# Scores of two query tiles in one group, and one PSUM bank each for the transposed probabilities and the value products

## The chip, the cores and the metric

The kernel runs on one core of a Trainium2 chip. A core has five engines that work from queues of their own: PE (TensorE: matrix products and transposes), DVE (VectorE), ACT (ScalarE), POOL (GpSimd) and SP (which issues DMAs). Each executes its instructions in order and waits on semaphores that the others raise. PE writes into PSUM, eight banks of 128 partitions by 512 float32 values; ACT and DVE read it. The metric is the device time of one execution in microseconds.

## The reference

One decoder layer on a sequence of 512 tokens and 1,024 channels. Of it the change touches the attention alone:

```python
ilog = einsum('bqhd,bsd->bqhs', qib, ki)                # indexer: which 128 keys a query keeps
_, sel = lax.top_k(iscore, topk)
s = einsum('bqhd,bqkhd->bhqk', qb, kg) * scale          # 8 heads of 64
s = s - slopes[None, :, None, None] * dist[:, None]     # ALiBi
p = jax.nn.softmax(s, axis=-1)
return einsum('bhqk,bqkhd->bqhd', p, vg)
```

Before it stand the modulated norm and the input projections, after it the gates, the output projection and a gated MLP.

## The kernel before

All large products are done in float32 parts: a weight is split by ACT into a high part (L805) and by POOL into a low part (L721), and a product is two high products and one low product for each block of 128 rows.

**The attention loop.** The 512 queries are four tiles of 128 (i = 0 to 3). Tile i sees (i + 1) x 128 keys. The heads are taken in four pairs. A step is one head and one tile; there are 32. The loop `for t in range(SLOTS)` stands in the programs of PE, ACT and DVE, and one turn of it is called a slot here. `ORDER` puts the steps of a pair as tile 0, 0, 1, 1, 3, 3, 2, 2, the two heads in turn. What one step needs is spread over slots:

- PE, slot t: at the first slot of a pair the scores of tiles 0 and 1 of both heads (twelve products), at its fifth those of tile 3 (six), at its seventh those of tile 2 (six). `scored_with` says which, and PE waits for `logit_ok` of step t-1 before them. A score product contracts over 64 rows, so the two heads of a pair take one half of the array each. Both heads' scores go to `SC`, banks 3 and 4.
- DVE, slot t: adds the scores to the linear term (L1419), which leaves the row's maximum; then the bias of the exponential (L1423); then, for step t-1, the division by the sum (L1430).
- ACT, slot t: the linear term of step t+1 (L979), the exponential of step t (L1010, which waits for the bias and, since `prob` has three places, for the transposes of step t-3), and the copy of the transposed probabilities of step t-3 from PSUM to `pT` (L1018).
- PE, slot t: transposes the probabilities of step t-3 (L1857), i + 1 of 128 x 128, into `PT[(t - 3) % 2]`, banks 5 and 6 in turn. It waits for the copy of step t-5, the last reader of that bank.
- PE, slot t, last: a filler, which is a part of a projection that has nothing to do with the step. Even slots do the high products and odd slots the low ones: 16 and 8 products of 512 columns for the fillers `gp` and `ga`, 8 and 4 for `pb`. Their banks are 0 and 1. The order is gp in slots 0 to 3, pb 4 to 7, gp 8 to 11, pb 12 to 15, gp 16 to 19, pb 20 to 27, ga from 28.
- ACT, at the end of every even slot: after the filler's last product, the high split of the weight three fillers ahead (L805) and, for gp and ga, a tanh (L926, L993).
- PE, slots 11, 19, 27 and 35: `head_products`, the value products of a pair, into `HEADS`, which is bank 7 (OB) for pairs 0 and 2 and bank 2 for pairs 1 and 3. They are read in the slot after by ACT (L1000) and DVE (L1278).

```python
HEADS = (OB, banks[2])
return {0: (0, 1), 4: (3,), 6: (2,)}.get(r, ())   # scored_with, r = t % 8
pe.wait_ge(pt_ok, t - 4)                          # before the transposes of slot t
```

Bank 2 belongs to the ring of banks of the projections before the loop (its last user is the first gp product) and after it. Bank 6 is also the last of the four that take the spread norm of the keys before the loop (`k_turn`, `kn_ok`).

Of the kernel before, what the change touches and what calls it, by code (L numbers as in the profile page):

```python
# [8 lines left out]
ACT = mybir.ActivationFunctionType  # L9
AX_X = mybir.AxisListType.X  # L10

P = 128
S, D, FF = 512, 1024, 2816
H, HD = 8, 64
# [4 lines left out]
NT = S // P  # L19
# [74 lines left out]
def scored_with(t):  # L94

    r = t % (2 * NT)
    return {0: (0, 1), 4: (3,), 6: (2,)}.get(r, ())


def scores_by(t):  # L100
# [5 lines left out]
def score_columns(i):  # L106

    return slice(P, 3 * P) if i == 1 else slice(0, (i + 1) * P)
# [163 lines left out]
def build_layer(nc, x, c, w_ada, b_ada, norm1_g, w_in, q_norm_g, k_norm_g, w_attn_br, w_pool_grp, pool_scale,  # L272
                w_pool_br, w_out, norm2_g, w_up, conv_w, conv_b, w_down, out):
    sch = schedule()
    drained_count = []
# [14 lines left out]
    with ExitStack() as ctx:  # L290
# [59 lines left out]
        qT = arena("qT", [P, 2, KA, S], F32R, 0)  # L350
        kT = arena("kT", [P, 2, KA, S], F32R, 16)
        vS = arena("vS", [P, NT, H, HD], F32, 32)
# [25 lines left out]
        logit = arena("logit", [P, 2, S], F32, 93)  # L378
# [27 lines left out]

        banks = [ctx.enter_context(nc.psum_tensor(f"bank{n}", [P, S], F32)) for n in range(8)]
        SC, PT, OB = banks[3:5], banks[5:7], banks[7]
        HEADS = (OB, banks[2])
        SUMS = ((OB, OB), SC)  # L410
        TURN = ((SC[1], PT[0]), (PT[1], OB))

        def gate_banks(n):

            return PT if n else (OB, banks[sch.bank[sch.chunk["wo", 1, 2]]])


        def accumulator(j):
            return {3: macc_rows, 4: macc_gain}.get(j, macc)
# [370 lines left out]
        def _(act):  # L790
# [205 lines left out]
            for t in range(SLOTS):  # L996
                if finished(t) is not None:
                    m = finished(t)
                    act.wait_ge(pv_ok, 2 * (m + 1))
                    me.did(act.activation(qT[:, 0, m, :], HEADS[m % 2][:, :], ACT.Copy), head_hi)  # L1000
                if t < STEPS:
                    if t + 1 < STEPS:
                        alibi_terms(t + 1)
                    h, i = step_of(t)
                    n = (i + 1) * P
                    act.wait_ge(bias_ok, t + 1)
                    if t >= 3:
                        act.wait_ge(prob_t, t - 2)
                    r = i * 2 * H + h
                    me.did(act.activation(prob[:, t % 3, 0:n], logit[:, t % 2, 0:n], ACT.Exp,  # L1010
                                          bias=sbias[:, t:t + 1], scale=stat[:, 2, r:r + 1],
                                          accum_out=ssum[:, t:t + 1]), exp_ok)
                if 3 <= t < STEPS + 3:
                    h, i = step_of(t - 3)
                    act.wait_ge(prob_t, t - 2)
                    if h >= 2:
                        act.wait_ge(pv_ok, 2 * (h // 2))
                    me.did(act.activation(pT[h % 2][:, 0:i + 1, i * P:(i + 1) * P],  # L1018
                                          PT[(t - 3) % 2][:, 0:(i + 1) * P].rearrange("p (j n) -> p j n", n=P),
                                          ACT.Copy), pt_ok)  # L1020
                if t and filler(t - 1)[1] == "low":
                    kind, m = filler(t - 1)[0]
                    if kind == "gp":
                        pool_gate(m)
                    if kind == "ga":
                        gate(m)
                    if kind == "pb":
                        chunk((kind, m))
# [121 lines left out]
        def _(dve):  # L1150
# [126 lines left out]
            def low_of(out_ap, full, hi, signal):  # L1277
                me.did(dve.tensor_tensor(out_ap, full, hi.bitcast(F32), ALU.subtract), signal)  # L1278
# [134 lines left out]
            for t in range(SLOTS):  # L1413
                if t < STEPS:
                    h, i = step_of(t)
                    n = (i + 1) * P
                    dve.wait_ge(linear, t + 1)
                    dve.wait_ge(score, scores_by(t))
                    me.did(dve.tensor_tensor_reduce(logit[:, t % 2, 0:n], logit[:, t % 2, 0:n], SC[t % 2][:, score_columns(i)],  # L1419
                                                    1.0, TAKEN, ALU.add, ALU.max, smax[:, t:t + 1]), logit_ok)  # L1420
                    me.settle()
                    r = i * 2 * H + h
                    me.did(dve.tensor_scalar(sbias[:, t:t + 1], smax[:, t:t + 1], stat[:, 2, r:r + 1], -1.0,  # L1423
                                             ALU.mult, ALU.mult), bias_ok)
                if 1 <= t < STEPS + 1:
                    n = (step_of(t - 1)[1] + 1) * P
                    dve.wait_ge(exp_ok, t)
                    me.did(dve.reciprocal(sinv[:, t - 1:t], ssum[:, t - 1:t]))
                    me.settle()
                    me.did(dve.tensor_scalar(prob[:, (t - 1) % 3, 0:n], prob[:, (t - 1) % 3, 0:n],  # L1430
                                             sinv[:, t - 1:t], None, ALU.mult), prob_ok)
                if finished(t) is not None:
                    m = finished(t)
                    dve.wait_ge(head_hi, m + 1)
                    low_of(qT[:, 1, m, :], HEADS[m % 2][:, :], qT[:, 0, m, :], head_lo)
                if t and filler(t - 1)[1] == "low" and filler(t - 1)[0][0] == "pb":
                    name = filler(t - 1)[0]
                    m = name[1]
                    await_chunk(dve, name)
                    dve.wait_ge(drained["act"], drained_count[sch.chunk["gp", m]][1])  # L1440
                    me.did(dve.scalar_tensor_tensor(out=ypool[:, m, :], in0=ypool[:, m, :], scalar=1.0,
                                                    in1=bank(name)[:, :], op0=ALU.add, op1=ALU.mult),
                           drained["dve"])
# [141 lines left out]
        def _(pe):  # L1585
# [228 lines left out]
            def head_products(m):  # L1814

                pe.wait_ge(pt_ok, 2 * NT * (m + 1))
                if m == 1:
                    who, n = drained_count[max(k for k in range(sch.chunk[FILLERS[0]]) if sch.bank[k] == 2)]
                    pe.wait_ge(drained[who], n)
                if m >= 2:  # L1820
                    pe.wait_ge(head_lo, m - 1)
                for j in range(NT):
                    for e in range(2):
                        mm = pe.matmul(HEADS[m % 2][e * HD:(e + 1) * HD, j * P:], vS[:, j, 2 * m + e, :],  # L1824
                                       pT[e][:, j, j * P:], start=j == 0, stop=j == NT - 1)
                        if j == NT - 1:
                            mm.then_inc(pv_ok, 1)

            for t in range(SLOTS - 1):
                if pair_products(t) is not None:  # L1830
                    head_products(pair_products(t))
                if t < STEPS and scored_with(t):

                    h = step_of(t)[0]
                    if t % (2 * NT) == 0:
                        pe.wait_ge(k_lo, h // 2 + 1)
                    if t == 0:
                        pe.wait_ge(kn_ok, 2)
                    else:
                        pe.wait_ge(logit_ok, t)  # L1840
                    for i in scored_with(t):
                        for a, b in THREE:
                            for e in range(2):
                                r = slice(e * HD, (e + 1) * HD)
                                mm = pe.matmul(SC[e][:, score_columns(i)], qT[r, a, h // 2, i * P:(i + 1) * P],  # L1845
                                               kT[r, b, h // 2, 0:(i + 1) * P], start=(a, b) == (0, 0), stop=a == 1)
                                if a == 1:
                                    mm.then_inc(score, 1)
                if 3 <= t < STEPS + 3:
                    i = step_of(t - 3)[1]  # L1850
                    pe.wait_ge(prob_ok, t - 2)
                    if t < 5:
                        pe.wait_ge(kn_ok, t)
                    else:
                        pe.wait_ge(pt_ok, t - 4)
                    for j in range(i + 1):
                        mm = pe.transpose(PT[(t - 3) % 2][:, j * P:(j + 1) * P],  # L1857
                                          prob[:, (t - 3) % 3, j * P:(j + 1) * P], ident[:, :])
                    mm.then_inc(prob_t, 1)
                if filler(t) and t < STEPS + 3:  # L1860
                    name, part = filler(t)
                    if part == "high":
                        await_bank(pe, name)
                    (high_products if part == "high" else low_products)(
                        sch.unit[name], bank(name), mix if name[0] == "pb" else hT)
# [123 lines left out]
```

## Time and profile before

| | |
|---|---|
| median of 3 runs | 734.26 us (734.16 to 734.49) |
| the profiled execution | 733.26 us |
| its span, first to last instruction | 731.4 us |
| PE busy | 715.4 us (98%) |
| DVE, ACT, POOL busy | 384.6, 307.1, 300.1 us |
| granted TensorE clock, mean | 0.997 of full speed |
| attention loop on PE | about 162.4 to 270.1 us of the span |

Busy PE is time between the start of a product and its modelled end; the gap from the start of one group to the start of the next says what the group really costs. In a timeline the first number is a start in us from the span's beginning, the second how long the group took, and a bracket holds the idle time before it and what ended it.

### The profile page before, as it was taken

The numbers are of one execution on the slowest core, as the hardware profiler recorded it, in microseconds if no ns is written. First come the engines' busy times: TensorE is split into PE (matmuls) and PEld (weight loads), VectorE is DVE, ScalarE is ACT, GpSimd is POOL, SyncE is SP. The second block draws the span as 40 slices with busy tenths as digits, with TensorE's granted clock in tenths as the row PEclk, the third lists the DMA queues.
The fourth block names the chain that finished last, engine by engine and source line by source line (L and its number), as shares of the span: only waits on it lengthen the run. The fifth ranks groups of instructions, "written<-read, shape, count | busy, mean of one in ns | idle before, by whom it ended". The sixth has DMA issues, their size and how long they took to land.

```text
span 731.4 us, 9316 instructions
## 1 busy us (share of the span) xinstructions
PE 715.4 (98%) x3440; PEld 577.6 (79%) x3440; DVE 384.6 (53%) x706; ACT 307.1 (42%) x507; POOL 300.1 (41%) x159
## 2 busy tenths in 40 slices
PE   5899999999999999999999999999999999999997
PEld 4667688877777778887898888887888888888886
DVE  3558899965366616798855445555434432004002
ACT  6325532567577633352636344343334343121120
POOL 1001448826242325473316445444334434445340
PEclk9999999999999999999999999999999999999999
DMA  9993321311311136495095244244243233142401
GB/s 320 357 392 116 120 68 58 115 58 59 113 60 59 59 100 257 150 318 182 3 333 154 61 114 115 63 111 115 58 116 109 64 115 116 32 147 81 144 0 58
DMA packets 87306, 92.73 MB, mean 127 GB/s; under 512 B 2275, under 2 KB 69599, under 8 KB 87263
## 3 DMA queue, kind: packets, MB, share of 16 engines
q1 hardware_dynamic: 84927, 83.23, 35.6%
q10 hardware_dynamic: 2336, 8.92, 3.3%
q8 instruction: 28, 0.46, 0.2%
q14 instruction: 15, 0.12, 0.1%
HBM read 90.05 MB, written 2.10 MB: 126 GB/s over the span
## 4 chain that ended last, share of the span: by engine, by line
PE 83%; DVE 14%; ACT 2%; issue 1%; POOL 0%; DVEq 0%; POOLq 0%; ACTq 0%
PE bank L1592 33%; PE bank L1612 21%; PE bank L1601 17%; PE bank L1662 4%; DVE work L1329 3%; DVE top L1326 3%; PE bank L1857 1%; PE bank L1845 1%; PE bank L1824 1%; PE bank L1644 1%; PE bank L1630 1%; DVE macc_rows L1191 1%; DVE full L1507 1%; DVE pmean L1360 1%; DVE pmean L1356 1%
## 5 line engine op out<-in xcount | busy, mean ns | idle before, releaser
L721 POOL TENSOR_TENSOR wsplit<-stage,wsplit 128x1024 fp32r<-128x1024 f32 (+1 forms) x113 | 259.6, 2300 | 384.7 <-ACT wsplit L805 326.3
L1592 PE MATMUL bank<-hT,wsplit 128*128 128x512 f32 (+1 forms) x1120 | 257.4, 382 | 0.4 <-DVE hT L1515 0.4
L1592 PEld LDWEIGHTS bank<-hT,wsplit 128*128 128x128 f32 x1120 | 203.2, 188 | 41.7 <-issue 1.3
L805 ACT ACTIVATE wsplit<-stage 128x1024 fp32r<-128x1024 f32 (+2 forms) x121 | 120.1, 994 | 251.0 <-PE bank L1601 166.3
L1601 PE MATMUL bank<-hT,wsplit 128*128 128x512 f32 (+1 forms) x560 | 134.5, 382 | 0.0
L1612 PE MATMUL bank<-wsplit,guT 128*128 128x512 f32 x528 | 119.8, 389 | 0.0
L1601 PEld LDWEIGHTS bank<-hT,wsplit 128*128 128x128 f32 x560 | 101.6, 188 | 19.6 <-issue 0.2
L1612 PEld LDWEIGHTS bank<-wsplit,guT 128*128 128x128 f32 x528 | 99.1, 188 | 20.5
L1550 DVE SCALAR_TENSOR_TENSOR yb<-bank,conv,yb 128x511 f32<-128x511 f32 (+1 forms) x44 | 32.9, 749 | 65.1 <-ACT yb L1125 64.4
L1550 DVE SCALAR_TENSOR_TENSOR ya<-bank,conv,ya 128x511 f32<-128x511 f32 (+1 forms) x44 | 33.0, 749 | 59.6 <-ACT ya L1125 58.8
L1475 DVE TENSOR_TENSOR tmp_last<-bank,gate_row 128x512 f32<-128x512 f32 x8 | 5.5, 688 | 101.7 <-PE bank L1612 101.7
L1662 PE MATMUL bank<-hT,wsplit 128*128 128x512 f32 x168 | 41.4, 403 | 2.0 <-ACT hT L837 2.0
L1662 PEld LDWEIGHTS bank<-hT,wsplit 128*128 128x128 f32 x168 | 32.0, 194 | 11.1 <-issue 4.5
L1010 ACT ACTIVATE prob<-logit,sbias,stat 128x128 f32<-128x128 f32 (+3 forms) x32 | 20.9, 652 | 26.9 <-PE bank L1857 17.7
L1419 DVE CUSTOM_DVE_ANT_0 logit<-logit,bank 128x128 f32<-128x128 f32 (+3 forms) x32 | 15.4, 482 | 30.4 <-PE bank L1845 25.7
L1612 PE MATMUL bank<-wsplit,hT 128*128 128x512 f32 x96 | 24.2, 400 | 0.0
L1329 DVE MATCH_REPLACE8 work<-top,work 128x256 f32<-128x256 f32 (+2 forms) x45 | 24.0, 543 | 0.0
L1430 DVE TENSOR_SCALAR prob<-prob,sinv 128x128 f32<-128x128 f32 (+3 forms) x32 | 22.5, 702 | 1.1
L1612 PE MATMUL bank<-wsplit,merged 128*128 128x512 f32 x96 | 22.5, 394 | 0.0
L1326 DVE MAX8 top<-work 128x8 f32<-128x256 f32 (+2 forms) x45 | 22.2, 549 | 0.5
L1612 PE MATMUL bank<-own,merged 128*128 128x512 f32 x96 | 22.4, 391 | 0.0
L1612 PEld LDWEIGHTS bank<-wsplit,hT 128*128 128x128 f32 x96 | 17.4, 188 | 5.7 <-issue 1.7
(193 smaller groups left out, 751.6 us busy)
## 6 DMA issues: line engine op xcount, KB each, us to landing
stage<-in_w_up_dram SPq DMA_DIRECT2D x44, 512.0 KB, 5.1
stage<-in_w_in_dram SPq DMA_DIRECT2D x14, 1024.0 KB, 5.2
stage<-in_w_down_dram SPq DMA_DIRECT2D x10, 1024.0 KB, 5.1
ada_first<-in_w_ada_dram SPq DMA_DIRECT2D x16, 512.0 KB, 9.1
ada_mid<-in_w_ada_dram ACTq DMA_DIRECT2D x8, 1024.0 KB, 7.8
ada_row<-in_w_ada_dram SPq DMA_DIRECT2D x8, 512.0 KB, 11.0
stage<-in_w_out_dram SPq DMA_DIRECT2D x4, 1024.0 KB, 7.0
ada_last<-in_w_ada_dram SPq DMA_DIRECT2D x4, 1024.0 KB, 10.9
```

The lines of the kernel that those rows point to most:

```text
L721: pool.tensor_tensor(unit_split(n, 1), unit_source(n), unit_split(n, 0).bitcast(F32), ALU.subtract).then_inc(low, 1)
L805: me.did(act.activation(unit_split(n, 0), unit_source(n), ACT.Copy), high)
L1010: me.did(act.activation(prob[:, t % 3, 0:n], logit[:, t % 2, 0:n], ACT.Exp, bias=sbias[:, t:t + 1], scale=stat[:, 2, r:r + 1], accum_out=s ...
L1326: found = [me.did(dve.max(top8[:, i, :], row_of(src, i))) for i in range(1, NT)]
L1329: me.did(dve.match_replace(out=row_of(work, i), in_to_replace=top8[:, i, :], in_values=row_of(src, i), imm_value=TAKEN))
L1419: me.did(dve.tensor_tensor_reduce(logit[:, t % 2, 0:n], logit[:, t % 2, 0:n], SC[t % 2][:, score_columns(i)], 1.0, TAKEN, ALU.add, ALU.max ...
L1430: me.did(dve.tensor_scalar(prob[:, (t - 1) % 3, 0:n], prob[:, (t - 1) % 3, 0:n], sinv[:, t - 1:t], None, ALU.mult), prob_ok)
L1550: me.did(dve.scalar_tensor_tensor(out=y[:, m % 2, back:], in0=bank((kind, m))[:, 0:S - back], scalar=w, in1=y[:, m % 2, back:], op0=ALU.mu ...
L1592: pe.matmul(out_bank[:, tokens], hi[:, k, :], rhs[:, part, k, tokens], start=k == 0 and part == 0, stop=False)
L1601: mm = pe.matmul(out_bank[:, tokens], lo[:, k, :], rhs[:, 0, k, tokens], start=False, stop=k == nk - 1)
L1612: mm = pe.matmul(out_bank[:, :], rows_of[:, a, k0 + r, t * P:(t + 1) * P], unit_split(n, b)[:, r, :], start=first and r == 0 and (a, b) == ...
L1662: mm = pe.matmul(bank(name)[:, :], unit_split(k, a)[:, 0, at:at + P], hT[:, part, k, :], start=start, stop=stop)
```

## The change

Tiles 3 and 2 are scored together, at the fifth slot of a pair: twelve products in one group. Tile 2 goes to the two banks of `SC`, tile 3 to banks 2 and 6. For this the value products of all pairs go to bank 7 and wait for the low part of the pair before, and all transposes go to bank 5 and wait for the copy of step t-4, made in the slot before. The waits that guard banks 2 and 6 against their earlier users are put before the first such group (t = 4).

```diff
--- before.py
+++ after.py
@@ -94,7 +94,7 @@
 def scored_with(t):
 
     r = t % (2 * NT)
-    return {0: (0, 1), 4: (3,), 6: (2,)}.get(r, ())
+    return {0: (0, 1), 4: (3, 2)}.get(r, ())
 
 
 def scores_by(t):
@@ -406,7 +406,7 @@
 
         banks = [ctx.enter_context(nc.psum_tensor(f"bank{n}", [P, S], F32)) for n in range(8)]
         SC, PT, OB = banks[3:5], banks[5:7], banks[7]
-        HEADS = (OB, banks[2])
+        WIDEST = (banks[2], PT[1])
         SUMS = ((OB, OB), SC)
         TURN = ((SC[1], PT[0]), (PT[1], OB))
 
@@ -414,6 +414,10 @@
 
             return PT if n else (OB, banks[sch.bank[sch.chunk["wo", 1, 2]]])
 
+
+        def score_bank(i, e):
+
+            return WIDEST[e] if i == NT - 1 else SC[e]
 
         def accumulator(j):
             return {3: macc_rows, 4: macc_gain}.get(j, macc)
@@ -997,7 +1001,7 @@
                 if finished(t) is not None:
                     m = finished(t)
                     act.wait_ge(pv_ok, 2 * (m + 1))
-                    me.did(act.activation(qT[:, 0, m, :], HEADS[m % 2][:, :], ACT.Copy), head_hi)
+                    me.did(act.activation(qT[:, 0, m, :], OB[:, :], ACT.Copy), head_hi)
                 if t < STEPS:
                     if t + 1 < STEPS:
                         alibi_terms(t + 1)
@@ -1016,7 +1020,7 @@
                     if h >= 2:
                         act.wait_ge(pv_ok, 2 * (h // 2))
                     me.did(act.activation(pT[h % 2][:, 0:i + 1, i * P:(i + 1) * P],
-                                          PT[(t - 3) % 2][:, 0:(i + 1) * P].rearrange("p (j n) -> p j n", n=P),
+                                          PT[0][:, 0:(i + 1) * P].rearrange("p (j n) -> p j n", n=P),
                                           ACT.Copy), pt_ok)
                 if t and filler(t - 1)[1] == "low":
                     kind, m = filler(t - 1)[0]
@@ -1416,7 +1420,7 @@
                     n = (i + 1) * P
                     dve.wait_ge(linear, t + 1)
                     dve.wait_ge(score, scores_by(t))
-                    me.did(dve.tensor_tensor_reduce(logit[:, t % 2, 0:n], logit[:, t % 2, 0:n], SC[t % 2][:, score_columns(i)],
+                    me.did(dve.tensor_tensor_reduce(logit[:, t % 2, 0:n], logit[:, t % 2, 0:n], score_bank(i, t % 2)[:, score_columns(i)],
                                                     1.0, TAKEN, ALU.add, ALU.max, smax[:, t:t + 1]), logit_ok)
                     me.settle()
                     r = i * 2 * H + h
@@ -1432,7 +1436,7 @@
                 if finished(t) is not None:
                     m = finished(t)
                     dve.wait_ge(head_hi, m + 1)
-                    low_of(qT[:, 1, m, :], HEADS[m % 2][:, :], qT[:, 0, m, :], head_lo)
+                    low_of(qT[:, 1, m, :], OB[:, :], qT[:, 0, m, :], head_lo)
                 if t and filler(t - 1)[1] == "low" and filler(t - 1)[0][0] == "pb":
                     name = filler(t - 1)[0]
                     m = name[1]
@@ -1814,14 +1818,11 @@
             def head_products(m):
 
                 pe.wait_ge(pt_ok, 2 * NT * (m + 1))
-                if m == 1:
-                    who, n = drained_count[max(k for k in range(sch.chunk[FILLERS[0]]) if sch.bank[k] == 2)]
-                    pe.wait_ge(drained[who], n)
-                if m >= 2:
-                    pe.wait_ge(head_lo, m - 1)
+                if m:
+                    pe.wait_ge(head_lo, m)
                 for j in range(NT):
                     for e in range(2):
-                        mm = pe.matmul(HEADS[m % 2][e * HD:(e + 1) * HD, j * P:], vS[:, j, 2 * m + e, :],
+                        mm = pe.matmul(OB[e * HD:(e + 1) * HD, j * P:], vS[:, j, 2 * m + e, :],
                                        pT[e][:, j, j * P:], start=j == 0, stop=j == NT - 1)
                         if j == NT - 1:
                             mm.then_inc(pv_ok, 1)
@@ -1838,23 +1839,27 @@
                         pe.wait_ge(kn_ok, 2)
                     else:
                         pe.wait_ge(logit_ok, t)
+                    if t == NT:
+                        pe.wait_ge(kn_ok, NT)
+                        who, n = drained_count[max(k for k in range(sch.chunk[FILLERS[0]]) if sch.bank[k] == 2)]
+                        pe.wait_ge(drained[who], n)
                     for i in scored_with(t):
                         for a, b in THREE:
                             for e in range(2):
                                 r = slice(e * HD, (e + 1) * HD)
-                                mm = pe.matmul(SC[e][:, score_columns(i)], qT[r, a, h // 2, i * P:(i + 1) * P],
+                                mm = pe.matmul(score_bank(i, e)[:, score_columns(i)], qT[r, a, h // 2, i * P:(i + 1) * P],
                                                kT[r, b, h // 2, 0:(i + 1) * P], start=(a, b) == (0, 0), stop=a == 1)
                                 if a == 1:
                                     mm.then_inc(score, 1)
                 if 3 <= t < STEPS + 3:
                     i = step_of(t - 3)[1]
                     pe.wait_ge(prob_ok, t - 2)
-                    if t < 5:
-                        pe.wait_ge(kn_ok, t)
+                    if t == 3:
+                        pe.wait_ge(kn_ok, 3)
                     else:
-                        pe.wait_ge(pt_ok, t - 4)
+                        pe.wait_ge(pt_ok, t - 3)
                     for j in range(i + 1):
-                        mm = pe.transpose(PT[(t - 3) % 2][:, j * P:(j + 1) * P],
+                        mm = pe.transpose(PT[0][:, j * P:(j + 1) * P],
                                           prob[:, (t - 3) % 3, j * P:(j + 1) * P], ident[:, :])
                     mm.then_inc(prob_t, 1)
                 if filler(t) and t < STEPS + 3:
```

## Rows read from the trace of the kernel before

**Rows 1.** Page, parts 1 and 4: busy time per engine; chain that ended last.
```profile
PE 715.4 (98%) x3440; PEld 577.6 (79%) x3440; DVE 384.6 (53%) x706; ACT 307.1 (42%) x507; POOL 300.1 (41%) x159
...
PE 83%; DVE 14%; ACT 2%; issue 1%; POOL 0%; DVEq 0%; POOLq 0%; ACTq 0%
```

**Rows 2.** Waits of PE; columns are total us, times, longest us.
```profile
PE bank L1845 <- DVE kraw L1368: 0.3, 1, 0.3
```

**Rows 3.** Timeline of PE, slots 12 to 16 (start us, us taken).
```profile
198.80 0.97 PE L1845 MATMUL bank<-kT,qT 64*128 64x512 f32 x6
199.69 0.33 PE L1857 MATMUL bank<-ident,prob 128*128 128x128 f32 x1
...
201.72 0.38 PE L1857 MATMUL bank<-ident,prob 128*128 128x128 f32 x2
201.85 1.17 PE L1601 MATMUL bank<-mix,wsplit 128*128 128x512 f32 x4
202.95 0.79 PE L1845 MATMUL bank<-kT,qT 64*128 64x384 f32 x6
203.67 0.44 PE L1857 MATMUL bank<-ident,prob 128*128 128x128 f32 x2
...
205.80 0.60 PE L1857 MATMUL bank<-ident,prob 128*128 128x128 f32 x4
...
208.15 0.66 PE L1857 MATMUL bank<-ident,prob 128*128 128x128 f32 x4
```

**Rows 4.** Timeline of ACT, slots 12 to 16.
```profile
200.89 0.82 ACT L1010 ACTIVATE prob<-logit,sbias,stat 128x512 f32<-128x512 f32 x1 [1.82 <-DVE sbias L1423]
...
201.70 0.26 ACT L1018 ACTIVATE pT<-bank 128x128 f32<-128x128 f32 x1
201.86 1.05 ACT L805 ACTIVATE wsplit<-stage 128x1024 fp32r<-128x1024 f32 x1
...
203.28 0.61 ACT L979 ACTIVATE logit<-dsel,alibi 128x384 f32<-128x384 f32 x1
203.79 0.81 ACT L1010 ACTIVATE prob<-logit,sbias,stat 128x512 f32<-128x512 f32 x1
...
204.59 0.37 ACT L1018 ACTIVATE pT<-bank 128x256 f32<-128x256 f32 x1
...
206.05 0.37 ACT L1018 ACTIVATE pT<-bank 128x256 f32<-128x256 f32 x1
...
208.25 0.59 ACT L1018 ACTIVATE pT<-bank 128x512 f32<-128x512 f32 x1
```

**Rows 5.** Timeline of DVE, its first logit step of slot 12.
```profile
199.91 0.69 DVE L1419 CUSTOM_DVE_ANT_0 logit<-logit,bank 128x512 f32<-128x512 f32 x1 [7.73 <-PE bank L1845]
```

**Rows 6.** Timeline of PE, transposes of slot 6.
```profile
179.50 0.44 PE L1857 MATMUL bank<-ident,prob 128*128 128x128 f32 x2
```

**Rows 7.** Timeline of PE, transposes of slots 22, 26 and 30.
```profile
227.84 0.44 PE L1857 MATMUL bank<-ident,prob 128*128 128x128 f32 x2
...
234.89 1.17 PE L1601 MATMUL bank<-mix,wsplit 128*128 128x512 f32 x4
235.90 0.49 PE L1857 MATMUL bank<-ident,prob 128*128 128x128 f32 x3
...
249.25 0.44 PE L1857 MATMUL bank<-ident,prob 128*128 128x128 f32 x2
```

**Rows 8.** Timeline of ACT, copies to pT in slots 5, 21, 25 and 29.
```profile
180.42 0.37 ACT L1018 ACTIVATE pT<-bank 128x256 f32<-128x256 f32 x1
...
228.33 0.37 ACT L1018 ACTIVATE pT<-bank 128x256 f32<-128x256 f32 x1
...
235.94 0.47 ACT L1018 ACTIVATE pT<-bank 128x384 f32<-128x384 f32 x1
...
247.68 0.36 ACT L1018 ACTIVATE pT<-bank 128x256 f32<-128x256 f32 x1
```

**Rows 9.** Windows: busy us (instructions) of PE, PEld, DVE, ACT, POOL, then PEclk.
```profile
20.00:24.00 4.00, 3.22 (x8) 2.60 (x9) 3.62 (x5) 1.89 (x3) 0.00 (x0) 0.57 1.09 359
```

## Prediction

> **What bounds the kernel.** I read the page first. PE is busy for 715.4 of 731.4 us, and the chain that ended last gives PE 83% [rows 1], so an edit counts only if it changes the time at which PE can go on. The waits of PE come next: at the score products PE waited once, 0.3 us in all [rows 2], and the list has no wait at the transposes. So in the attention stage (162 to 270 us) PE goes from one product to the next; whatever is put between them arrives at the end in full, since after it PE runs as densely and nothing there could absorb it. Then I laid the timelines of PE and ACT side by side for each pair of heads. I call one turn of the loop over t a slot; the transposes in slot t are those of step t-3, and ACT copies them to pT in its own slot t, after that slot's exponential.
>
> **What is removed.** Slot 6 of every pair (t = 6, 14, 22, 30) no longer begins with six score products: those of tile 2 now follow tile 3 in slot 4. The products are not fewer. What goes is the edge of a group. Six products of 512 columns take 0.89 us to the next operation (198.80 to 199.69), six of 384 columns 0.72 (202.95 to 203.67) [rows 3]. They run as three pairs, so 0.17 us for 3 x 128 columns is 0.057 per 128; three pairs of 512 cost 0.68 and three of 384 cost 0.51, and each group has 0.21 us more that belongs to no column. One group of twelve: 0.89 + 0.51 = 1.40 us, 0.21 saved. Going into a score group costs too: four low products take 1.10 us before one (201.85 to 202.95) and 1.01 before transposes (234.89 to 235.90) [rows 3, 7]. That is 0.09 more: 0.30 us a pair of heads, 1.2 us in all.
>
> **What is costed at nothing.** The head products all go to OB now, and wait for the low part of the pair before, written a slot after that pair's products, seven slots before the next pair's. At t = 4 the added waits (kn_ok, the drain of bank 2) are for readers that stand ahead of the loop in the code, four slots of fillers earlier. The wait of slot 4 for logit t-1 is unchanged, and tile 3 still goes first, so the first logit step of slot 12 starts as before, 1.11 us after the products do (198.80, 199.91) [rows 3, 5]. The second group's scores come sooner, but DVE needs ACT's linear term for them first, which is the later of the two. No DMA is issued or moved; the weight splits on ACT keep their order.
>
> **What is added.** The transposes of slot t write the one bank that the copy of slot t-1 reads, so PE must wait for the copy that ACT makes in the slot just before. With two banks it waited for the one before that. Behind that wait stand, on PE, the slot's filler products and everything later. ACT's work in a slot is long where a slot of PE is short. In slot 12 ACT starts the exponential at 200.89, on DVE's bias; a copy, a 1.05 us weight split and a tanh follow, the next linear term comes at 203.28, the exponential of slot 13 at 203.79, and its copy ends at 204.59 + 0.37 = 204.96 [rows 4]. That chain hangs on the scores of tile 3 and not on PE's later products: the transposes that the copy reads are over by about 202.6 even when moved by 0.51. So the copy still ends at 204.96. PE has transposed in slot 14 at 203.67 [rows 3], and would be ready at 203.67 - 0.30 = 203.37. It must now wait until 204.96.
>
> To this comes what PE takes to start again. No row shows PE woken by ACT here; the bounds are nothing and the 0.3 us of [rows 2], which holds a whole wait. I take 0.1, since ACT itself begins within about 0.1 us of what it waits for.
>
> The shift of a pair is read directly, as new start minus old start of the transposes in slot 6. It already contains the 0.30 us saved, which only lengthens the wait.
> - Pair 0: 180.42 + 0.37 + 0.1 - 179.50 = 1.39 us [rows 6, 8]
> - Pair 1: 204.96 + 0.1 - 203.67 = 1.39 us [rows 3, 4]
> - Pair 2: 228.33 + 0.37 + 0.1 - 227.84 = 0.96 us [rows 7, 8]. It is less because the split in it is half as wide.
> - Pair 3: the copy ends at 247.68 + 0.36 = 248.04, the transposes start at 249.25 [rows 7, 8]; its fillers are long, so no wait, and the saving shows: -0.30 us.
> - Slot 26: transposes at 235.90, the copy before them ends at 235.94 + 0.47 = 236.41 [rows 7, 8]. Both follow that pair's scores, so both move along with the pair: 236.41 + 0.1 - 235.90 = 0.61 us.
>
> Two transposes after scores took 0.44 us and 0.38 without [rows 3], 0.06 three times, -0.18. Sum: 1.39 + 1.39 + 0.96 + 0.61 - 0.30 - 0.18 = 3.87 us.
>
> **Where the stall goes.** Slots 7 and 8 would overlap too: in pair 1 transposes start at 205.80 and 208.15, the copies before them end at 206.05 + 0.37 = 206.42 and 208.25 + 0.59 = 208.84 [rows 3, 4]. But PE now arrives 1.39 later, at 207.19 and 209.54. The copies move less. Slot 14's exponential must await that slot's transposes, over at 205.06 + 0.44 = 205.50, so its copy ends near 206.7. In slot 15 they are over at 207.19 + 0.60 = 207.79; 0.1 for ACT's start, 0.80 from an exponential to its copy (203.79 to 204.59) and 0.59 for the copy give 209.28. Margins: 0.5 and 0.26 us. So one wait a pair, and the one margin is thin.
>
> The Trainium skill, page "Perfetto Trace Analysis", section Optimizing Tensor Performance, Matmuls, says that independent groups should rotate through PSUM banks so that the evacuation of one overlaps the next. It speaks against this change: by it every slot loses the overlap. By the rows only slots whose copy is late do, four of 32; were it every overlap that the rows of slots 14 to 16 show, unabsorbed, pair 1 alone would cost 1.29 + 0.62 + 0.69 = 2.6 us.
>
> **Rivals.**
> - The chain closes on itself (transposes, exponential, copy, transposes). If ACT needs 0.3 to 0.5 us more than I took in slots 7 and 8, the 0.26 margin is gone and each pair adds 0.1 to 0.8 us. With three pairs, +4.5 to +6.5 us, about 738.7 to 740.8. For: the thin margin. Against: PE's lateness gives ACT time.
> - The wait is hidden, the change pays. PE would have to find the copy done, so ACT would have to end it 204.96 - 203.37 = 1.6 us sooner. Then only the saving is left: -1.2 us, 733.1. That decides if the scores of tile 3 reach DVE much sooner from fresh banks, or if ACT's split in slot 12 is not in front of the exponential. Against: [rows 4] show ACT without a gap from 200.89 to the copy.
> - Part is hidden: ACT 0.8 us sooner in each pair, about half of each wait left, +1.2 us, 735.5.
> - The clock. PE's granted clock was 0.57 in a stretch of 4 us (so partly at 1.2 GHz) [rows 9] after PE had idled much of the start. A fall costs 4.00 x 0.43 = 1.7 us. If each of the four waits brought one, +6.9 on top, about 745. Against: each wait of 1.7 us or less lies in 20 us of solid products.
>
> The Trainium skill, page "TensorE: Matmul & The Clock Gate", section A second HAM failure mode: psum-queue depth-cycling, tells of such a kernel, with small idles between groups that let the clock fall. No row of the attention stage shows a fall, since it has no such idles yet.
>
> **Numbers.** The profiled execution took 733.26 us (span 731.4 and 1.9 around it), 1.0 below the median of 734.26; I add the 3.87 to the median: 738.1. A measurement can tell 0.2%, 1.5 us. The forecast's own range: restarts at 0 (-0.4), no wait in slot 26 (-0.6) and ACT 0.3 us sooner in three pairs (-0.9) give +2.0; restarts at 0.3 (+0.8) and ACT 0.2 later (+0.6) +5.3; so 736.2 to 739.6. Chances: forecast 0.75, closed chain 0.10, clock 0.03, part hidden 0.04, hidden 0.08. The range given reaches 0.2 further for part of the closed chain, and leaves out less than 0.2. Slower by over 0.2%: 0.75 + 0.10 + 0.03 and 0.01 of the part hidden, 0.89. Same: 0.03 of the part hidden and 0.06 of the hidden (-1.2 us is 0.17%), 0.09. Faster: 0.02.
>
> **What the profile after should show.** PE idle before L1857, released by ACT's copies (L1018), about 1.7, 1.7 and 1.3 us in slots 6, 14 and 22 and 0.6 in slot 26, none in slot 30; twelve score products in 1.4 us in slot 4; the first logit step still 1.1 us after them; the granted clock at 1.00 throughout. I am wrong if the copy of slot 5 ends sooner than 4.0 us after the first exponential of slot 4 starts, if slots 7 and 8 wait as well, or if PE loses no time in slot 6.

## The result, and the profile after

| | before | after |
|---|---|---|
| median | 734.21 us (733.57 to 734.49, 4 runs) | 738.04 us (737.79 to 738.43, 4 runs) |
| profiled execution | 733.26 us | 737.79 us |
| span | 731.4 us | 735.9 us |
| first score product to last value products (starts) | 162.45 to 265.87: 103.42 us | 162.87 to 270.37: 107.50 us |

The ratio is 1.0056, 95% interval 1.0044 to 1.0068. The change made the kernel 3.8 us slower by the medians (the interval of the ratio is 3.2 to 5.0 us); 3.87 was predicted. Between the two profiled executions there are 4.5 us, of which 0.42 lie ahead of the first score product. There the programs are the same, so I read the change from the stage itself, 4.08 us longer. Lines of the kernel are numbered a few higher in the profile after: L1862 are the transposes (L1857 before), L1850 the score products, L1022 the copies to pT.

The page after, parts 1 and 4, has the same 715 us of PE work as [rows 1] in a longer span, and the chain now passes less through PE:

```profile
PE 715.3 (97%) x3440; PEld 578.4 (79%) x3440; DVE 382.7 (52%) x706; ACT 307.9 (42%) x507; POOL 299.7 (41%) x159
...
PE 80%; DVE 14%; ACT 3%; issue 1%; POOL 0%; ACTq 0%; DVEq 0%; POOLq 0%
```

PE's waits (total us, times, longest) show what [rows 2] did not: four waits at the transposes for ACT's copies. In such a bracket or row the name behind the arrow is what ended the wait.

```profile
PE bank L1862 <- ACT pT L1022: 4.7, 4, 1.5
...
PE bank L1850 <- DVE kraw L1372: 0.3, 1, 0.3
```

The timeline of PE in pair 1, slots 12 to 16, answers to [rows 3]:

```profile
200.55 1.50 PE L1850 MATMUL bank<-kT,qT 64*128 64x512 f32 x12
201.98 0.33 PE L1862 MATMUL bank<-ident,prob 128*128 128x128 f32 x1
...
204.01 0.38 PE L1862 MATMUL bank<-ident,prob 128*128 128x128 f32 x2
204.14 1.17 PE L1605 MATMUL bank<-mix,wsplit 128*128 128x512 f32 x4
206.86 0.41 PE L1862 MATMUL bank<-ident,prob 128*128 128x128 f32 x2 [1.54 <-ACT pT L1022]
...
208.96 0.60 PE L1862 MATMUL bank<-ident,prob 128*128 128x128 f32 x4
...
210.42 0.95 PE L1850 MATMUL bank<-kT,qT 64*128 64x128 f32 x12
211.30 0.66 PE L1862 MATMUL bank<-ident,prob 128*128 128x128 f32 x4
```

The twelve score products take 201.98 - 200.55 = 1.43 us. The transposes of slot 14 start at 206.86, and the bracket says why. The four low products ahead of them began at 204.14 and last 1.01 us, so PE stood from about 205.15 to 206.86, 1.71 us. The bracket's 1.54 counts from the modelled end of the last product.

The timeline of ACT for the same slots, beside [rows 4]:

```profile
202.65 0.82 ACT L1014 ACTIVATE prob<-logit,sbias,stat 128x512 f32<-128x512 f32 x1 [1.82 <-DVE sbias L1427]
...
203.46 0.25 ACT L1022 ACTIVATE pT<-bank 128x128 f32<-128x128 f32 x1
203.62 1.05 ACT L809 ACTIVATE wsplit<-stage 128x1024 fp32r<-128x1024 f32 x1
...
205.04 0.60 ACT L983 ACTIVATE logit<-dsel,alibi 128x384 f32<-128x384 f32 x1
205.55 0.80 ACT L1014 ACTIVATE prob<-logit,sbias,stat 128x512 f32<-128x512 f32 x1
...
206.34 0.37 ACT L1022 ACTIVATE pT<-bank 128x256 f32<-128x256 f32 x1
...
207.37 0.71 ACT L1014 ACTIVATE prob<-logit,sbias,stat 128x384 f32<-128x384 f32 x1
...
208.07 0.36 ACT L1022 ACTIVATE pT<-bank 128x256 f32<-128x256 f32 x1
```

From the exponential of slot 12 to the copy of slot 13 it is the chain of before, 1.75 to 1.76 us later throughout (202.65 for 200.89, 206.34 for 204.59): exponential, copy, split of 1.05 us, tanh, linear term, exponential, copy. The copy ends at 206.34 + 0.37 = 206.71 and PE goes on at 206.86, 0.15 after it. The split starts before PE stands and ends before the copy does; within these rows nothing on ACT waits. DVE's first logit step of slot 12 starts 201.66 - 200.55 = 1.11 us after the scores, as in [rows 5]:

```profile
201.66 0.69 DVE L1423 CUSTOM_DVE_ANT_0 logit<-logit,bank 128x512 f32<-128x512 f32 x1 [7.73 <-PE bank L1850]
```

Transposes of slots 6, 22 and 26, and of slot 30 (PE, two stretches of the timeline), beside [rows 6, 7]; 239.02 is the filler ahead of slot 26:

```profile
181.30 0.41 PE L1862 MATMUL bank<-ident,prob 128*128 128x128 f32 x2 [1.55 <-ACT pT L1022]
...
232.00 0.41 PE L1862 MATMUL bank<-ident,prob 128*128 128x128 f32 x2 [1.11 <-ACT pT L1022]
...
239.02 1.17 PE L1605 MATMUL bank<-mix,wsplit 128*128 128x512 f32 x4
```

```profile
240.69 0.52 PE L1862 MATMUL bank<-ident,prob 128*128 128x128 f32 x3 [0.49 <-ACT pT L1022]
...
253.81 0.38 PE L1862 MATMUL bank<-ident,prob 128*128 128x128 f32 x2
```

Slot 30 has no bracket: no wait in pair 3. The window of the stage (PE, PEld, DVE, ACT and POOL busy, then the granted clock) has the clock at 1.00 in spite of the waits:

```profile
162.87:274.00 111.13, 106.43 (x574) 80.25 (x575) 52.80 (x174) 69.77 (x163) 40.66 (x23) 1.00 0.21 67
```

### The profile page after: what moved, and what is told of

It reads as the page before. It is cut to its first block, busy times and chain, and to the rows that moved or that the text cites. A ratio compares the mean times of both kernels' runs of the same rounds, so it can differ in the third digit from the quotient of the medians.

```text
span 735.9 us, 9317 instructions
## 1 busy us (share of the span) xinstructions
PE 715.3 (97%) x3440; PEld 578.4 (79%) x3440; DVE 382.7 (52%) x706; ACT 307.9 (42%) x507; POOL 299.7 (41%) x159
## 4 chain that ended last, share of the span: by engine, by line
PE 80%; DVE 14%; ACT 3%; issue 1%; POOL 0%; ACTq 0%; DVEq 0%; POOLq 0%
PE bank L1596 32%; PE bank L1616 21%; PE bank L1605 16%; PE bank L1666 4%; DVE work L1333 3%; DVE top L1330 3%; PE bank L1825 1%; PE bank L1862 1%; PE bank L1850 1%; PE bank L1648 1%; PE bank L1634 1%; DVE macc_rows L1195 1%; DVE full L1511 1%; ACT wsplit L809 1%; DVE pmean L1364 1%
## 5 line engine op out<-in xcount | busy, mean ns | idle before, releaser
L1616 PEld LDWEIGHTS bank<-wsplit,merged 128*128 128x128 f32 x96 | 18.0, 188 | 4.2 <-issue 0.5
```

Of the source, the lines that this page charges most:

```text
L1616: mm = pe.matmul(out_bank[:, :], rows_of[:, a, k0 + r, t * P:(t + 1) * P], unit_split(n, b)[:, r, :], start=first and r == 0 and (a, b) == ...
```

## The experiments

My theory: the whole loss is PE's wait for the copy of the slot just before, which one bank for the transposes forces; the longer score group saves 0.30 us a pair (the edge of a group, that is what a group costs beyond its columns), and the value products in one bank cost nothing. The rivals were that the grouping, the fresh banks or the shared bank 7 cost something themselves, and that a group's edge costs nothing. Times are medians; the ratio is to runs of the kernel before on the same chip. "Stage" is from the first score product to the start of the last value products in the profiled execution.

| kernel | us | kernel before, same chip | ratio (95%) | stage |
|---|---|---|---|---|
| before | 734.21 | | | 103.42 |
| changed | 738.04 | 734.21 | 1.0056 (1.0044 to 1.0068) | 107.50 |
| e1, transposes take turns with bank 7 | 733.09 | 733.72 | 0.9984 (0.9976 to 0.9993) | 102.28 |
| e2, changed, two groups | 738.41 | 733.72 | 1.0053 (1.0041 to 1.0065) | 107.95 |
| e3, before, value products in bank 7 | 733.56 | 733.72 | 0.9993 (0.9983 to 1.0003) | 103.42 |
| e5, before, one group more a pair | 735.47 | 733.72 | 1.0020 (1.0011 to 1.0028) | 104.89 |
| e4, changed, split after the copy | 736.75 | 733.63 | 1.0038 (1.0024 to 1.0051) | 105.85 |
| e6, e1 with two groups | 735.51 | 733.63 | 1.0018 (1.0008 to 1.0028) | 104.67 |

The stage falls into five parts, from one score group to the next (us, in the profiled executions; the last part ends at the last value products):

| kernel | slots 0 to 3 | 4 to 11 | 12 to 19 | 20 to 27 | 28 to the end |
|---|---|---|---|---|---|
| before, and e3 | 12.18 | 24.17 | 24.16 | 18.70 | 24.21 |
| changed | 12.12 | 25.56 | 25.57 | 20.34 | 23.91 |
| e1 | 12.14 | 23.82 | 24.04 | 18.39 | 23.89 |
| e2 | 12.14 | 25.68 | 25.58 | 20.35 | 24.20 |
| e5 | 12.72 | 24.47 | 24.47 | 19.01 | 24.22 |
| e4 | 12.18 | 24.98 | 24.97 | 19.83 | 23.89 |
| e6 | 12.15 | 24.60 | 24.59 | 19.12 | 24.21 |

Slots 0 to 3 are the same work in all of them but e5, and take 12.12 to 12.18, so a difference under about 0.1 us in a part says little.

**e1: take the wait away, keep the grouping.** Bank 7 holds value products only in the slots t % 8 = 3 and 4. Against the changed kernel:

```diff
+        def turn_bank(t):
+            return OB if t % (2 * NT) in (0, 2, 6) else PT[0]
...
-                    else:
+                    elif t < 6 or t % (2 * NT) in (4, 5):
                         pe.wait_ge(pt_ok, t - 3)
+                    else:
+                        pe.wait_ge(pt_ok, t - 4)
+                    if t > 2 * NT + 4 and t % (2 * NT) == 6:
+                        pe.wait_ge(head_lo, t // (2 * NT))
                     for j in range(i + 1):
-                        mm = pe.transpose(PT[0][:, j * P:(j + 1) * P],
+                        mm = pe.transpose(turn_bank(t)[:, j * P:(j + 1) * P],
```

> The changed kernel, with one thing mended: in the slots t % 8 = 0, 2 and 6 the transposes go to bank 7 (OB), which holds value products only in the slots t % 8 = 3 and 4, and in the other slots to bank 5. So the transposes of slots 6, 7, 8 and 26 wait again for the copy made two slots before. My theory (the loss is the wait for the copy of the slot just before, and the saving of 0.30 us a pair is real): PE has no wait released by ACT's copies, and 734.2 - 1.2 = 733.0 us. Rival (the grouping, the fresh banks or the value products in one bank cost something themselves, the wait being only where it shows): 735 us or more.

Measured: 733.09 us, and a stage of 102.28 us, 5.22 shorter than the changed kernel's and 1.14 shorter than before's. All PE waits for copies are gone. PE in slots 13 to 16, and ACT's copy that is in question:

```profile
202.27 1.18 PE L1609 MATMUL bank<-mix,wsplit 128*128 128x512 f32 x4
203.29 0.38 PE L1870 MATMUL bank<-ident,prob 128*128 128x128 f32 x2
...
205.70 1.17 PE L1609 MATMUL bank<-mix,wsplit 128*128 128x512 f32 x4
207.02 0.96 PE L1854 MATMUL bank<-kT,qT 64*128 64x128 f32 x12 [0.16 <-DVE smax L1427]
```

```profile
204.49 0.37 ACT L1026 ACTIVATE pT<-bank 128x256 f32<-128x256 f32 x1
```

PE starts the transposes of slot 14 at 203.29, while the copy of slot 13 runs until 204.49 + 0.37 = 204.86, 1.57 us later. That overlap is what the one bank forbade. The only bracket is 0.16 us at slot 16, for DVE's logits: the four low products ahead of that group take 207.02 - 205.70 = 1.32 us to it, against 1.10 before, so slot 16 lost 0.22 us. The grouping and the fresh banks are here in full and the stage is shorter than before's, so they cost nothing that shows: the rival falls. The interval of the ratio lies below 1. The medians differ by 0.6 us and the ratio says 1.2; the stage says 1.14, near the 1.2 expected. By parts it gains 0.35, 0.12, 0.31 and 0.32 us; with the 0.22 of slot 16 added back, the second is 0.34. So a merged group saves 0.31 to 0.35 us, a little more than 0.30, and the new wait for the logits takes the excess away.

**e2: keep the one bank, undo the grouping.**

```diff
-    return {0: (0, 1), 4: (3, 2)}.get(r, ())
+    return {0: (0, 1), 4: (3,), 6: (2,)}.get(r, ())
```

> The changed kernel with its banks, but tile 2 is scored at the seventh slot of a pair again, in a group of its own. My theory: in pairs 0 to 2 PE goes on when the copy of slot 5 has ended, whatever it did before, so the products and the edge of the group lie inside the wait; only pair 3, which has no such wait, is 0.3 us later. 738.1 + 0.3 = 738.4 us, with the wait at slot 6 shorter by about 1 us in pairs 0 to 2. Rival (wait and saving simply add): 738.1 + 1.2 = 739.3 us.

Measured: 738.41 us, a stage 0.45 us longer than the changed kernel's. From the scores of slot 12 to those of slot 16 it takes 9.86 us, against 9.87 (200.55 to 210.42) in the changed kernel: six products put in the way again, and one hundredth moves. Pair 0, slots 4 to 11, is 0.12 longer, of which 0.10 lie between the transposes of slots 6 and 7; no run says why. Pair 3, from its slot 28 on, is 0.29 longer (247.02 to 271.22, against 246.46 to 270.37). PE in slots 13 and 14:

```profile
204.39 0.41 PE L1862 MATMUL bank<-ident,prob 128*128 128x128 f32 x2 [0.23 <-ACT pT L1022]
...
205.66 0.80 PE L1850 MATMUL bank<-kT,qT 64*128 64x384 f32 x6
207.39 0.41 PE L1862 MATMUL bank<-ident,prob 128*128 128x128 f32 x2 [0.94 <-ACT pT L1022]
```

The wait of slot 6 is shorter, but by 0.6 us and not the 1 I wrote, since PE comes to slot 5 half a microsecond sooner and waits there as well (0.23 in its bracket). The sum is what counts: PE goes on when the copy has ended. A saving ahead of a wait is worth nothing.

**e3: the value products in one bank, alone.**

```diff
-        HEADS = (OB, banks[2])
+        HEADS = (OB, OB)
...
-                if m >= 2:
-                    pe.wait_ge(head_lo, m - 1)
+                if m:
+                    pe.wait_ge(head_lo, m)
```

> The kernel before with one part of the change: the value products of all pairs in bank 7, waiting for the low part of the pair before. My theory: no wait, 734.2 us, the same. Rival (the second bank hid something at the value products): 0.5 us a pair for pairs 1 to 3, 735.7 us.

Measured: 733.56 us, ratio 0.9993 with 1 inside the interval, and the stage is 103.42 us, the same to the hundredth, as is each of its parts. It costs nothing.

**e5: twice the suspected cost of a group's edge,** with no bank changed.

```diff
-    return {0: (0, 1), 4: (3,), 6: (2,)}.get(r, ())
+    return {0: (0,), 2: (1,), 4: (3,), 6: (2,)}.get(r, ())
...
-    r = t % (2 * NT)
-    return t - r + 4 if r < 4 else t + 1
+    return t + 1
```

> The kernel before with one score group more in each pair: tile 0 alone at the first slot and tile 1 alone at the third. It doubles the suspected cost of a group's edge. My theory: 0.30 us for each of four more groups, 734.2 + 1.2 = 735.4 us, with no new wait. Rival (the edge overlaps with what stands beside it, so a group costs only its products): 734.2 us.

Measured: 735.47 us, a stage 1.47 us longer and no new wait. The mean is 0.37 us for each group more, but the parts from slot 4 on are 0.30, 0.31, 0.31 and 0.01 longer, and slots 0 to 3 alone 0.54. The group of tile 0 alone in slot 16:

```profile
206.00 0.44 PE L1856 MATMUL bank<-ident,prob 128*128 128x128 f32 x2
...
209.59 0.55 PE L1844 MATMUL bank<-kT,qT 64*128 64x128 f32 x6
210.07 0.66 PE L1856 MATMUL bank<-ident,prob 128*128 128x128 f32 x4
```

Six products of 128 columns take 210.07 - 209.59 = 0.48 us to the next operation; twelve of 128 and 256 took 0.89 in the kernel before. The three later groups cost the 0.30 that was expected. The first is dearer, and 0.24 us of it is the way in: eight low products took 1.81 us to the next filler before (167.14 to 168.95), and 2.05 to the new score group in e5 (168.24 to 170.29). No transposes stand beside those fillers yet; that this is what makes the edge dearer is likely, but no run tests it. The rival (it overlaps) falls.

**e4: is it the split that stands before the copy, or all of ACT's chain?** Against the changed kernel, in pairs 0 to 2:

```diff
+                if t % (2 * NT) == 5 and t < 2 * NT * 3:
+                    high_parts(sch.unit[filler(t - 2)[0]] + 1 + NRING)
                 if t and filler(t - 1)[1] == "low":
                     kind, m = filler(t - 1)[0]
                     if kind == "gp":
-                        pool_gate(m)
+                        pool_gate(m, t % (2 * NT) != 4)
```

With the second argument false `pool_gate` leaves its own split out.

> The changed kernel; in pairs 0 to 2 the weight split that ACT makes in slot 4 (0.95 us of ACT's time in pairs 0 and 1, 0.52 in pair 2) comes after the copy of slot 5 instead of ahead of it. If only the place of the split sets the wait, 2.4 us come back: 735.6 us. My theory is narrower: with one bank the transposes, the exponential and the copy of slots 4 to 8 follow each other on ACT with hardly a gap, and the transposes of slot 8 were ready only 0.2 us after their copy. So the wait of slot 6 shrinks by 0.95 us, and slots 7 and 8 now wait for most of it: 0.2 us a pair is left, 737.4 us.

Measured: 736.75 us, ratio 1.0038; the stage is 1.65 us shorter than the changed kernel's. That lies between the two: not the 2.4 that moving the split should bring by itself, and over twice the 0.6 that I gave it. PE in slots 14 and 15, and ACT from the copy of slot 13:

```profile
205.48 0.41 PE L1865 MATMUL bank<-ident,prob 128*128 128x128 f32 x2 [0.60 <-ACT pT L1023]
205.64 2.10 PE L1599 MATMUL bank<-mix,wsplit 128*128 128x512 f32 x8
207.89 0.63 PE L1865 MATMUL bank<-ident,prob 128*128 128x128 f32 x4
```

```profile
204.96 0.37 ACT L1023 ACTIVATE pT<-bank 128x256 f32<-128x256 f32 x1
...
206.17 0.61 ACT L984 ACTIVATE logit<-dsel,alibi 128x384 f32<-128x384 f32 x1
206.68 0.71 ACT L1015 ACTIVATE prob<-logit,sbias,stat 128x384 f32<-128x384 f32 x1
```

The wait of slot 6 fell from 1.54 to 0.60. Of the 0.94, PE gave back 0.31 in slot 7: eight high products take 1.94 us (207.02 to 208.96 in the changed kernel), so PE was ready at 205.64 + 1.94 = 207.58 and the transposes start at 207.89. From the scores of slot 12 to those of slot 16 it is 9.25 us for 9.87 in pair 1, 0.62 less. I had taken the chain on ACT as closed, with 0.2 us to give. It had more. In slot 7 of the changed kernel PE came 0.38 us after it could have gone on (the copy ends at 208.07 + 0.36, and 0.15 more is 208.58, against 208.96), and the chain had a gap: there ACT's linear term of slot 14 was done at about 207.12 and the exponential began at 207.37, for it waits for the transposes that PE was late with. Here it follows the linear term at once (206.17, 206.68). The gap of 0.25 us and the 0.38 make the 0.62 up to a hundredth. So the direction held (slot 7 waits again), the size did not.

**e6: e1 with two groups,** to have the price of an edge with the same banks on both sides. Its edit is that of e2.

> The mended kernel (transposes in bank 7 in slots 0, 2 and 6, else bank 5), but with tile 2 scored at the seventh slot again. No wait for ACT's copies here either, so this is the plain price of the group's edge, with four score banks in both: 733.1 + 1.2 = 734.3 us, and the stage from the first score product to the last value products as long as before, 103.4 us. Rival (part of the gain of the mended kernel came from the fresh banks): less than 103.0 us.

Measured: 735.51 us and a stage of 104.67, so neither my 103.4 nor the rival's. The reason is a wait that I had not seen, in slot 5 of pairs 0 to 2:

```profile
PE bank L1870 <- ACT pT L1026: 0.7, 3, 0.2
```

With six products in slot 4 and not twelve, PE comes to slot 5 about 0.54 us sooner (0.89 for 1.43), and slot 5 still has the wait for the copy of slot 4. In pair 1 the transposes of slot 13 start 203.76 - 200.45 = 3.31 us after the scores, and 201.72 - 198.80 = 2.92 in [rows 3]: 0.39 us, three times 1.2. Of the 104.67 - 102.28 = 2.39 us to e1, 1.2 is this; with the 0.22 that e1 lost in slot 16, 1.4 is left for four edges. In pairs 0 to 2 the edge is spoiled as a measurement, since it needs that subtraction. Pair 3 has no wait in either kernel: 24.21 - 23.89 = 0.32 us for the edge. And 24.21 is what the kernel before takes there, so the fresh banks by themselves gained nothing.

## Why the prediction was right

- **The sum.** Against before the parts are longer by: slots 0 to 3 -0.06 (0 predicted), pair 0 from slot 4 +1.39 (1.33), pair 1 +1.41 (1.33), pair 2 +1.64 (0.90 + 0.61 = 1.51), pair 3 -0.30 (-0.30). Together 4.08 against 3.87. Two terms were mis-sized. PE needed 0.15 us after the copy's end (206.71 to 206.86), where I took 0.1: four times 0.05. And the 0.06 that the transposes were to take less, three times, was about 0.03: after a wait two transposes are neither the 0.44 of a pair behind scores nor the 0.38 of a pair without, but 0.41, and the transposes of slot 15 shift by 208.96 - 205.80 = 3.16 where those of slot 14 shift by 206.86 - 203.67 = 3.19.
- **The number.** That the medians differ by 3.83, four hundredths from the forecast, is luck: the stage missed by 0.21, the interval of the ratio is 3.2 to 5.0 us, and the profiled executions are 4.5 apart.
- **The group's edge,** 0.30 us a pair: 0.30 in pair 3, 0.31 to 0.35 in e1, 0.32 in pair 3 of e6, 0.30 and 0.31 in the later groups of e5 and 0.54 in its first. Shown, for groups that stand between transposes and fillers. Its make-up was a little off: a group of twelve took 1.43 us against 1.40 worked out, so 0.18 was saved behind it and not 0.21, and the 0.06 of the transposes, which the prediction kept apart, belongs to the same saving.
- **The wait,** 1.69 us worked out for slots 6 and 14, from 203.37 to 205.06: 1.71 measured; in slot 26 PE stood from 239.02 + 1.01 = 240.03 to 240.69, 0.66 for 0.61. That the bank is its cause is shown by e1, which gives the transposes a second bank, with the wait that guards bank 7, and changes nothing else.
- **Costed at nothing:** the value products (e3) and the four score banks (e1, and pair 3 of e6) did cost nothing that shows.
- **The stall goes no further.** Slots 7 and 8 do not wait in the changed kernel. The margin of 0.26 us at slot 8 held: the copy of slot 15 ends at 210.93 and PE comes at 211.30, so 0.22 us are left beyond the 0.15 that PE needs.
- **The rivals.** The closed chain did not happen, though e4 shows it near: take 0.94 us from the wait of slot 6 and slot 7 begins to wait. The clock stayed at 1.00 over the stage with four waits of up to 1.7 us in it. The Trainium skill's page "TensorE: Matmul & The Clock Gate", section A second HAM failure mode: psum-queue depth-cycling, has idles between groups that let it fall, and no run here shows that. That a wait of this length is harmless everywhere is not shown either: at about 19 to 21 us all eight traces have a PE wait of 1.96 us, and in seven of them the granted clock fell beside it (last section). The Trainium skill's page "Perfetto Trace Analysis", section Optimizing Tensor Performance, Matmuls, has groups rotate through banks. The trace agrees in the slots where the copy is late (slot 6 in three pairs, and slot 26), and in the other slots the rotation was worth nothing.

## What to carry to other kernels

Before a double buffer is given up, lay the reader's end beside the writer's next start, slot by slot, and not on average: of 32 slots four lost anything here, and these lost 5.4 us (1.7, 1.7, 1.3 and 0.7), over four times the 1.2 that the change saved. A saving that ends in a wait is worth nothing (e2), and a wait that is shortened at one place comes back in part at the next when the releasing engine's chain is nearly closed (e4). A bank that is in use for two slots of eight is a second buffer for the other six: with it the same grouping gains 1.1 us in the stage where it lost 4.1 (e1).

## What the runs showed that I had not expected

The stage's length repeats closely where nothing in it changed (103.42 us in before and in e3), while the time ahead of it does not. Its programs are the same in all eight kernels, and yet the first score product starts at 160.29 us in e3 and at 163.94 in e5, 3.65 us later. The windows of the first 60 us, e3 first and then e5 (the last three figures are the granted clock, the DMA share and GB/s):

```profile
0.00:60.00 60.00, 49.27 (x269) 36.33 (x270) 32.19 (x60) 25.48 (x42) 3.10 (x18) 1.00 0.98 344
```

```profile
0.00:60.00 60.00, 49.17 (x253) 36.11 (x254) 28.52 (x56) 23.16 (x40) 2.73 (x17) 0.94 0.99 344
```

The granted clock was 1.00 of full speed in the one and 0.94 in the other. The timeline of PE says where this counts, again e3 and then e5:

```profile
19.95 5.04 PE L1662 MATMUL bank<-hT,wsplit 128*128 128x512 f32 x21 [1.96 <-ACT hT L837]
```

```profile
20.93 7.73 PE L1661 MATMUL bank<-hT,wsplit 128*128 128x512 f32 x21 [1.96 <-ACT hT L836]
```

The same 21 products take 2.69 us longer, with the granted clock at 0.58 from 20 to 28 us in e5 and at 1.00 in e3. The other 0.98 us of the difference is there before they start: 0.85 of it in 32 transposes that take 5.29 us in e3 and 6.14 in e5, both from 8.00 us on and both with the clock given as 1.00. Why they differ is open. (60 x 0.06 = 3.6 us looks like the whole difference, but it also counts the fall while PE still stood, up to 20.93 us, and the products lost 2.69.) In 20 to 40 us the clock was 0.91 in before, changed, e1 and e4, 0.85 in e2, 0.83 in e5 and e6, and 1.00 in e3 alone, each time behind the same wait of 1.96 us; what decides it no run here shows. So in this kernel a difference of a microsecond between single executions says nothing of the attention stage. Compare the stage, or enough runs.
